# Value projection with 512 features per matmul over four PSUM banks, and linear attention begun one weight unit later

## What is computed

```python
# 4 heads, DK = 128, DV = 256, chunks of 64 positions; v is (tokens, 1024)
def step(s, inp):
    qd, ki, ke, vc, tot = inp
    att = jnp.where(lower_tri, jnp.einsum('bhtd,bhsd->bhts', qd, ki), 0.0)
    o = jnp.einsum('bhts,bhsv->bhtv', att, vc) + jnp.einsum('bhtd,bhdv->bhtv', qd, s)
    s = jnp.exp(tot[..., 0, :])[..., None] * s + jnp.einsum('bhsd,bhsv->bhdv', ke, vc)
    return s, o
```

## Time and profile before

| what | value |
|---|---|
| median of 3 runs | 1911.14 us (1909.93 to 1915.75) |
| the profiled execution | 1914.12 us, of which 1912.2 us are the span from the first to the last instruction |
| TensorE busy | 1849.8 us, 97% of the span |
| VectorE, ScalarE busy | 1344.5 us, 979.2 us |
| granted TensorE clock, mean | 0.993 of full speed |
| linear attention, layer 0 and layer 1 | about 72 to 218 us and 1217 to 1342 us |
| softmax attention, layer 0 and layer 1 | about 218 to 404 us and 1342 to 1477 us |

### The profile page before, as it was taken

The page is one execution under the profiler, slowest core; times in us unless marked ns, Lnnn a source line. Parts: engine busy times, 40 slices in busy tenths (PEclk is TensorE's granted clock), DMA queues, the critical chain, the costliest instruction groups (busy, mean ns, idle before and its releaser), DMA issues.

```text
span 1912.2 us, 26001 instructions
## 1 busy us (share of the span) xinstructions
PE 1849.8 (97%) x10464; PEld 1538.7 (80%) x10464; DVE 1344.5 (70%) x1954; ACT 979.2 (51%) x1397; POOL 39.4 (2%) x86
## 2 busy tenths in 40 slices
PE   8999999999999999999999998999999999989997
PEld 4778777777777887678888886888778888979997
DVE  4666546535677887879988787756657688678874
ACT  4543355545655323654344335543545887466653
POOL 1000010000000000000000000000100000000000
PEclk9999999999999999999999999999999999999999
DMA  8212222223243555234544563212323544635653
GB/s 339 74 56 62 78 72 67 80 81 99 89 143 132 182 187 184 80 105 165 174 155 146 199 210 126 78 58 78 105 80 106 161 155 150 187 121 179 186 179 119
DMA packets 69656, 249.80 MB, mean 131 GB/s; under 512 B 8336, under 2 KB 9376, under 8 KB 69408
## 3 DMA queue, kind: packets, MB, share of 16 engines
q1 hardware_dynamic: 65600, 235.96, 37.7%
q0 software_dynamic: 3360, 10.08, 1.8%
q10 hardware_dynamic: 576, 2.10, 0.3%
HBM read 244.44 MB, written 1.05 MB: 128 GB/s over the span
## 4 chain that ended last, share of the span: by engine, by line
PE 73%; DVE 17%; ACT 6%; issue 3%; POOL 0%; ACTq 0%; DVEq 0%; POOLq 0%
PE ps L1531 53%; DVE wlo L854 4%; PE ps L1521 4%; PE ps L1561 3%; DVE fa L904 2%; ACT whi L454 2%; PE ps L1801 2%; PE ps L1887 2%; PE ps L1822 1%; DVE state L1237 1%; PE ps L1739 1%; DVE xc L904 1%; PE ps L1717 1%; PE ps L1813 1%; PE ps L1678 1%
## 5 line engine op out<-in xcount | busy, mean ns | idle before, releaser
L854 DVE TENSOR_TENSOR wlo<-wraw,whi 128x1024 fp32r<-128x1024 f32 x352 | 429.6, 1222 | 239.1 <-ACT whi L454 238.7
L454 ACT ACTIVATE whi<-wraw 128x1024 fp32r<-128x1024 f32 x352 | 370.4, 1054 | 224.2 <-PE ps L1531 211.8
L1531 PE MATMUL ps<-hh,whi 128*128 128x512 f32 (+1 forms) x1632 | 367.3, 347 | 6.2 <-DVE fa L904 3.2
L1531 PE MATMUL ps<-hl,whi 128*128 128x512 f32 (+1 forms) x1632 | 363.1, 344 | 0.0
L1531 PE MATMUL ps<-hh,wlo 128*128 128x512 f32 (+1 forms) x1632 | 334.6, 346 | 1.9 <-DVE wlo L854 1.9
L1531 PEld LDWEIGHTS ps<-hh,whi 128*128 128x128 f32 x1632 | 268.9, 190 | 47.9 <-issue 6.3
L1531 PEld LDWEIGHTS ps<-hl,whi 128*128 128x128 f32 x1632 | 270.2, 190 | 37.3 <-issue 1.6
L1531 PEld LDWEIGHTS ps<-hh,wlo 128*128 128x128 f32 x1632 | 262.5, 190 | 40.9 <-issue 4.4
L882 DVE SCALAR_TENSOR_TENSOR ps<-wada,cond 128x1024 f32<-128x1024 f32 x144 | 173.5, 1246 | 0.0
L904 DVE SCALAR_TENSOR_TENSOR fa<-ps,par,fa 128x510 f32<-128x510 f32 (+1 forms) x176 | 100.1, 610 | 11.4 <-ACT fa L534 9.8
L1531 PE MATMUL ps<-bh,whi 128*128 128x512 f32 (+1 forms) x384 | 88.7, 353 | 0.0
(11 more groups left out here) (301 smaller groups left out, 2590.5 us busy)
## 6 DMA issues: line engine op xcount, KB each, us to landing
wraw<-in_weights SPq DMA_DIRECT2D x352, 512.0 KB, 3.6
wada<-in_w_ada_rows SPq DMA_DIRECT2D x80, 512.0 KB, 3.6
ada_first<-in_w_ada SPq DMA_DIRECT2D x14, 512.0 KB, 15.9
wgate<-in_w_gate POOLq DMA_DIRECT2D x16, 256.0 KB, 2.9
q_turned<-aq POOLq DMA_DIRECT2D x32, 64.0 KB, 2.3
x<-in_xt ACTq DMA_DIRECT2D x2, 512.0 KB, 7.6
x<-in_xt SPq DMA_DIRECT2D x2, 512.0 KB, 7.1
ada_first<-in_w_ada ACTq DMA_DIRECT2D x2, 512.0 KB, 12.4
```

The source lines that it names most:

```text
L454: A_(whi[u % HI][:], wraw[RING_W[u] % RAW][:], ACT.Copy).then_inc(s_hi, 1)
L854: V.tensor_tensor(wlo[s][:], wraw[s][:], whi[u % HI][:].bitcast(F32), ALU.subtract).then_inc(s_lo, 1)
L1531: ins = mm(dst[:, r, c:], w[:, kk, r * P:(r + 1) * P], x_[:, UK * h + kk, c:], start=h == 0 and k in (0, 2) and kk == 0, stop=h == m - 1 a ...
```

## The change

The four pairs of values become two groups of two pairs. In a group each of four units holds two tiles of input rows by 512 features instead of four tiles by 256 (`wide_units`), still 512 KB. One matmul moves 512 features into a whole bank; a unit has 24 matmuls, six parts of four, and the four token tiles of a group fill all four banks. Within a unit the token tiles 0 and 1 are worked in parts 0 to 2 (two parts with the high weights, one with the low), tiles 2 and 3 in parts 3 to 5. So the low half of the weights is wanted at part 2 instead of part 4, the second pair of banks at part 3 of the group's first unit (a new wait), and the first pair of banks is complete after part 2 of the group's last unit: a new semaphore, `s_rows`, lets ScalarE take it out there. For that edge ScalarE splits the next weights first and empties the pair behind it.

The order of the pairs becomes gqk 0, gqk 1, gv 0 and 1, gqk 2, gqk 3, gv 2 and 3, akv 0, akv 1, with all else as before. A head's `gla_kv` waits for both pairs of its group. The loop of the heads starts at u0+7; the part of the softmax attention that follows starts one unit later too, and as the units in front of `g1` are then one fewer, its filler ends after 114 parts instead of 120 (`fill`). The core of the diff:

```diff
-PAIR_ORDER = ([("gqk", 0), ("gqk", 1), ("gv", 0), ("gqk", 2), ("gv", 1), ("gqk", 3), ("gv", 2), ("akv", 0), ("gv", 3),
+PAIR_ORDER = ([("gqk", 0), ("gqk", 1), ("gv", 0), ("gv", 1), ("gqk", 2), ("gqk", 3), ("gv", 2), ("gv", 3), ("akv", 0),
...
+        elif _n == "gv":
+            UNIT += [(_l, _n, _i + _h % 2, _h, _q + _h % 2) for _h in range(4)] if _i % 2 == 0 else []
...
-                wait_pair_used(act, q)
+                if name == "gv" and i % 2 == 0:
+                    act.wait_ge(s_rows, 2 * l + i // 2 + 1)
+                else:
+                    wait_pair_used(act, q)
...
-                if q >= 0:
+                early = q >= 0 and UNIT[u - 1][1] == "gv" and UNIT[u - 1][2] % 2 == 0
+                if q >= 0 and not early:
                     evac_first(q)
                 if u + LEAD < NU and u + LEAD not in LATE:
                     hi(u + LEAD)
-                if q >= 0:
+                if early:
+                    evac_first(q)
+                elif q >= 0:
                     evac_second(q)
...
-                ua = first_unit(l, "aq", 1)
+                ua = first_unit(l, "aq", 1) + 1
...
-                if k == 4:
+                if k == (2 if name == "gv" else 4):
                     pe.wait_ge(s_lo, u + 1)
...
+                if name == "gv":
+                    if k == 3 and h == 0 and q >= 1:
+                        pe.wait_ge(taken[1], (q + 1) // 2)
+                    low = k % 3 == 2
+                    w = (wlo[s] if low else whi[u % HI])[:].rearrange("p (a b) c -> p a (b c)", a=2)
+                    for r in (2 * (k // 3), 2 * (k // 3) + 1) if low else (2 * (k // 3) + k % 3,):
+                        for x_ in (x_hi,) if low else (x_hi, x_lo):
+                            for kk in range(2):
+                                ins = mm(ps[:, r], x_[:, 2 * h + kk, r * P:(r + 1) * P], w[:, kk],
+                                         start=h == 0 and kk == 0 and not low and x_ is x_hi, stop=h == 3 and low and kk == 1)
+                    if h == 3 and k == 2:
+                        ins.then_inc(s_rows, 1)
...
-                parts(u0 + 4, 0, 12)
+                parts(u0 + 4, 0, 18)
                 for h in range(HEADS):
-                    u = u0 + 6 + 4 * h
+                    u = u0 + 7 + 4 * h
...
+                fill = 6 * (first_unit(l, "g1") - ub)
...
-                        parts(ub, b + 10, b + 13)
-                        parts(ub, b + 13, min(b + 15, 15 * AQ))
+                        parts(ub, b + 10, min(b + 15, fill))
```

More of the change, by code:

```diff
@@ L257, in build @@
         s_round, s_rowc = sem("ada_rounds_done"), sem("ada_rows_copied")
+        s_rows = sem("value_rows_half_done")
         s_red, s_ada = sem("ada_columns_done"), sem("ada_columns_taken")
@@ L689, in _ @@
                 edge(u0 + 5)
+                edge(u0 + 6)
                 for h in range(HEADS):
-                    u = u0 + 6 + 4 * h
+                    u = u0 + 7 + 4 * h
                     edge(u)
@@ L765, in _ @@
                                 edge(v)
-                        elif not even:
+                        elif not even and v + 1 < first_unit(l, "g1"):
                             edge(v + 1)
@@ L774, in _ @@
                             edge(v + 2)
-                    if l and not even:
+                    if l and not even and v + 1 < first_unit(l, "g1"):
                         edge(v + 1)
@@ L1377, in _ @@
                             edge(v)
-                        if k != first and not even:
+                        if k != first and not even and v + 1 < first_unit(l, "g1"):
                             edge(v + 1)
@@ L1510, in part @@
                     ready(l, name, i, h)
-                if k == 4:
+                if k == (2 if name == "gv" else 4):
                     pe.wait_ge(s_lo, u + 1)
                 w = whi[u % HI] if k < 4 else wlo[s]
-                if name == "gv" or (name, i) == ("akv", 1):
+                if name == "gv":
[10 more added lines that the diff above has]
+                        ins.then_inc(s_rows, 1)
+                elif (name, i) == ("akv", 1):
                     rows = (k,) if k < 4 else (2 * k - 8, 2 * k - 7)
@@ L1771, in _ @@
                         decays(h + 1)
[L1772 to L1775, removed]
+                    wait_pair_taken(pe, l, "gv", h // 2 * 2)
+                    wait_pair_taken(pe, l, "gv", h // 2 * 2 + 1)
                     gla_kv(h, 0)
@@ L1859, in _ @@
                         transposes(k + 1)
-                        parts(ub, b + 7, b + 10)
+                        parts(ub, b + 7, min(b + 10, fill))
                         att_out(k + 1)
-                        parts(ub, b + 10, b + 13)
-                        parts(ub, b + 13, min(b + 15, 15 * AQ))
+                        parts(ub, b + 10, min(b + 15, fill))
                     else:
@@ L1872, in _ @@
                             tile_stat(AKV + h + 2, 7)
-                        parts(ub, b + 5, min(b + 11, 15 * AQ))
-                        parts(ub, min(b + 11, 15 * AQ), min(b + 15, 15 * AQ))
+                        parts(ub, b + 5, min(b + 15, fill))
                 def lru_gates(n):
@@ L1918, in units, with wide_units @@
     return np.concatenate(got)
+def wide_units(w):
+    v = w.reshape(-1, 2, P, w.shape[1] // TOK, TOK).transpose(3, 0, 2, 1, 4)
+    return v.reshape(-1, P, UK, UC)
 def lay_out(inputs):
@@ L1938, in lay_out @@
             "gqk": units(w_in, [np.concatenate([tile(q0, h), tile(k0, h)]) for h in range(HEADS)]),
-            "gv": units(w_in, pair(v0)[:4]), "r": units(w_in, pair(r0)[:4]), "aq": units(w_in, pair(aq0)[:4]),
+            "gv": wide_units(w_in[:, v0:r0]), "r": units(w_in, pair(r0)[:4]), "aq": units(w_in, pair(aq0)[:4]),
             "akv": units(w_in, pair(ak0)[:2]), "lx": units(w_in, pair(lx0)[:4]), "y": units(w_in, pair(y0)[:4]),
@@ L1946, in lay_out @@
         for _, name, i, h, _ in (v for v in UNIT if v[0] == l):
-            u = UNITS_OF(name) * i + h
+            u = 4 * (i // 2) + h if name == "gv" else UNITS_OF(name) * i + h
             weights.append(parts[name][u:u + 1])
```

7 lines of the change are left out of this document (3 added, 4 removed).

## The result

The changed kernel takes 1923.18 us (median of 4 runs, 1921.44 to 1924.25) against 1910.54 for the kernel before: a ratio of 1.0063, 95% interval 1.0049 to 1.0077. It is slower by 12.6 us. The forecast was 1912.0, 1905 to 1918.

The account below looks back on a forecast made before the run. TensorE, busy 1849.8 of 1912.2 us, was taken as the bound, with VectorE or ScalarE setting the pace in places. The -5.1 and the other terms summed to +1.1: 1915.3 for the profiled execution, 1912 median, range 1905 to 1918.

Parts of the forecast that it names:

- The wide matmuls, -5.1: Values of both layers: 16 units go from 5.76 to 5.44 us each on TensorE, saving 5.1.
- The stretches, +1.0 and +1.8: First to last gla_kv, heads 0 to 2: VectorE's 13.67 us stands, giving back 1.0 in layer 0, 1.8 in layer 1.
- head 3, +1.1: Linear attention, layer 1: with ten short parts the stretch takes about 9.7 where filler alone makes 8.56, +1.1.
- The softmax attention of layer 0, +1.25 in three terms: Wait before the last output +1.35, an r pair ahead of out_hi +0.8, no aq pair ahead of the first square -0.9.
- "At nothing", the new wait at part 3: TensorE's wait for a gqk pair taken out during the three parts ahead, 2.7 against 1.2: no cost.
- The softmax attention of layer 1, +1.1: Around heads 4 and 5, some 5 and 3.5 us of new waits, less earlier waits and 0.4: +1.1.
- the credit for waits of before: Softmax attention of layer 1: earlier waits that go, 4.9 in the rows and about 2 hidden in modelled ends.
- the first square: Softmax attention of layer 1: it starts without the aq pair ahead of it, 0.4 us less.
- The first: Rival, the gain stays: fixed stretches are shorter or attention waits go, most of -5.1 remains, 1906; chance 0.24.
- the last two: Rivals on wide matmuls: 240 ns each saves nothing, 1917; or overhead of 2.5 ns saves 1.0, 1916; chance 0.04 each.
- The second: Rival, VectorE's lx pair in head 4 of layer 1: 8.5 added whole, about 1918; chance 0.12.

Follow-up runs that it names:

- e9: c1 with two matmuls moving 256 features for each that moves 512: 1913.4 us, 4.4 above c1.
- e1: The changed kernel with ScalarE emptying the second gqk pair ahead of the decay operations instead of behind them: 1916.6 us against 1923.2.
- e6: The changed kernel with one part more between the last two gla_kv of each linear attention head, taken from behind the head's output: 1916.9 us.
- e7: The changed kernel with four unread matmuls in layer 1, ahead of the wait for the last lx pair and of the scores behind it: 1922.0 us.
- e3: The kernel before, narrow matmuls and own pair order, with linear and softmax attention begun one unit later: 1916.8 us against 1909.9.
- e4: The changed kernel with VectorE rotating and norming the query tile ahead of the lx pair in head 4 of layer 1: 1919.8 us.
- e8: e1 with six parts instead of twelve between layer 1's two attentions, so its pairs stand beside the heads as in the kernel before: 1913.1 us.
- c1: The changed kernel with the edits of e1, e4 and e6 and weights split ahead of layer 1's r pairs: 1908.9 us against 1911.1 before.
- c3: c1 with unread matmuls at all three waits over 1 us in layer 1's softmax attention: 1908.4 us.
- e2: The changed kernel with each matmul of the values that moves 512 features cut into two that move 256: 1923.9 us against 1923.2.

## Why the prediction was wrong

- *The wide matmuls, -5.1: right.* 5.44 a unit. Of the 5.1, 4.2 arrive by the stages of e9; 0.6 of the rest is missing between the first gla_kv and the softmax attention, where TensorE waits for VectorE.
- *The stretches, +1.0 and +1.8, and head 3, +1.1: right.* With the bank waits gone (e1), the first value to the softmax attention changed by -1.5 in layer 0 and -0.1 in layer 1 against the kernel before, one unit added to it; the terms, with -2.6 a layer for the matmuls, give -1.6 and +0.3. e6 shows the cause.
- *The softmax attention of layer 0, +1.25 in three terms: near.* It is +1.85, with 1.11 of wait before the last output, as this row shows, and waits of 2.1 for out_lo behind two pairs of r where 1.3 stood before.

```profile
402.26 1.99 PE L1843 MATMUL ps<-probT,av 128*128 128x256 f32 x8 [1.11 <-ACT probT L743]
```

- *"At nothing", the new wait at part 3: wrong, +4.0.* This step failed first. It set 2.7 us of cover against a copy of 1.2 and left out that ScalarE does the decays, 3.4, ahead of that copy. The order of ScalarE's list shows it, and e1 gave the 4.0 back; I compared the durations and not the place.
- *The softmax attention of layer 1, +1.1: wrong, +7.6* (one unit that now lies ahead of the stage taken into account). The three waits came where the forecast had them, 6.9 in all of the 8.5 said. Two things made the rest. The low clock behind the waits was in no term: 1.75 at the scores, 0.5 at the transposes and 1.3 behind the wait for weights, each read against the same instructions of e7, and 1.2 behind the second scores, by the stage against e1: 4.8. And the credit for waits of before was 6.9 and 0.4 for the first square, which is already in the rows; the rows that go make 4.3. 6.9 - 4.3 + 4.8 is 7.4. That is a sum of places and not what runs give back: e7 takes the first three away and layer 1 is 2.8 shorter, not 3.55, because its last scores then wait 0.69 for the rotation. With 2.8 + 1.2 = 4.0 for the clock the account is 6.6, and 1.0 of the 7.6 has no shown cause. e3 shows that the later start alone brings these waits, e4 and e7 what of the loss is wait and what is clock, and e8 that the waits of before return with the old places.
- *The rivals.* The first fell with the 13.67 of the stretches, the last two with the 5.44 of a unit. The second had the place and the mechanism, and with 1918 lay nearest; it too had neither the clock nor the bank wait. The upper end of the range was its time, so the true one fell outside.

With +4.0 for nothing and +7.6 for +1.1 the sum, 1911.1 + 1.15, becomes 1922.8. It takes the start and the stage between the layers as equal, which in the two profiles they are not (3.4 us together), so that it meets the median so closely is in part luck.

What stays open: why one wait of 2.1 to 2.5 us brings the low clock and the same wait in a sister kernel does not. c1 to c3 show only that it moves.

## What to carry to other kernels

When a matmul is made to want a bank or a weight earlier, read what stands ahead of the instruction that frees it on that engine's own list; the duration of that instruction says little. A shift by one unit moves every evacuation beside every chain downstream, and its price is the waits it makes, plus the clock behind them. A saving on TensorE arrives only where TensorE sets the pace: of 5.1 us by the distances some 3.0 arrived in the changed kernel (e2, by its stages) and 4.2 with several of the waits gone (e9), and the time of the change shows neither.

## What the runs showed of the hardware

I had not expected waits of 2.1 to 2.5 us to cost 4.0 us more in clock (2.8 by e7, 1.2 by e1): 0.57 of full clock in the 8 us from 1448 on, with two of them just before and in it, and 1.00 with these waits filled. Nor that stages with the same instructions differ by 3.9 us (786.3 to 790.2) from one kernel to the next, with the low clock falling in other places, as the granted clock from 735 to 755 and from 795 to 830 us shows: between kernels that differ by 1 to 3 us the stage that was changed has to be compared, beside the time.
